# Attention in steps of four units instead of two, with eight probability buffers and one bank of sums

## What is computed

```python
def banded_attention(q, k, v, window, tab, sinks):
    ...
    logits = jnp.einsum('bgrnqd,bgnkd->bgrnqk', qb, kb).astype(jnp.float32) * (HEAD_DIM ** -0.5) + bias
    logits = jnp.where(valid, logits, NEG_INF)
    if sinks is None:
        probs = jax.nn.softmax(logits, axis=-1)
    ...
    out = jnp.einsum('bgrnqk,bgnkd->bgrnqd', probs.astype(v.dtype), vb)
```

## Time and profile before

| | |
|---|---|
| median of 3 runs | 4164.07 us (4163.08 to 4174.41) |
| the profiled execution | 4164.84 us, span 4162.8 us |
| PE, DVE, ACT busy over the span | 81%, 41%, 23% |
| granted PE clock, mean | 0.89 of 2.4 GHz |
| the five attention stages together | 414.5 us (A 99.1, B 41.5, C 52.4, S 110.2 and 111.3) |

### The profile page before, as it was taken

How to read it: one execution, slowest core, us unless ns; L and a number is a source line. 1 busy time by engine, 2 the same in 40 slices (tenths; PEclk the granted TensorE clock), 3 DMA queues, 4 the chain that set the end, 5 groups by cost and what they waited for, 6 DMA issues and landing times. The chain is left out here.

```text
span 4162.8 us, 48331 instructions
## 1 busy us (share of the span) xinstructions
PE 3381.5 (81%) x14856; PEld 2129.1 (51%) x14857; DVE 1702.3 (41%) x3938; ACT 966.0 (23%) x2034; POOL 326.0 (8%) x252
## 2 busy tenths in 40 slices
PE   4776859998997458996899999635789779999985
PEld 3644536666786326663444444413466534444443
DVE  2483553225342584225222222345832342222224
ACT  2263433223231223212111111012421301111111
POOL 0000000000000050000111111002300001111110
PEclk7788879999999678998899999867889989999997
DMA  3201011221312523310999999741422139999974
GB/s 119 80 1 67 26 48 46 89 81 54 114 65 67 179 101 92 81 36 35 372 403 406 400 394 400 287 156 41 152 57 86 51 127 412 399 404 392 386 292 181
DMA packets 286480, 747.29 MB, mean 180 GB/s; under 512 B 25475, under 2 KB 167181, under 8 KB 230132
## 3 DMA queue, kind: packets, MB, share of 16 engines
q1 hardware_dynamic: 258676, 677.81, 43.0%
q0 software_dynamic: 27648, 67.51, 4.1%
HBM read 719.71 MB, written 58.72 MB: 187 GB/s over the span
## 5 line engine op out<-in xcount | busy, mean ns | idle before, releaser
L2261 PE MATMUL up_ps<-experts,x_turned 128*64 128x512 f32 (+1 forms) x2256 | 696.7, 622 | 27.6 <-DMA experts<-in_w_up_dram 27.4
L2261 PEld LDWEIGHTS up_ps<-experts,x_turned 128*64 128x64 f32 (+1 forms) x2256 | 262.2, 160 | 385.0 <-issue 384.6
L242 DVE TENSOR_TENSOR pieces_lo<-weights,pieces_hi 128x512 fp32r<-128x512 f32 (+1 forms) x412 | 273.1, 683 | 329.3 <-ACT pieces_hi L236 327.6
L236 ACT CAST pieces_hi<-weights 128x512 fp32r<-128x512 f32 (+1 forms) x412 | 244.4, 614 | 463.4 <-PE products L254 102.2
L2285 PE MATMUL y_ps<-experts,hid_turned 128*64 128x512 f32 (+1 forms) x1128 | 345.6, 601 | 1.6 <-ACT hid_turned L2342 1.6
L2420 DVE TENSOR_TENSOR hid_seats<-up_ps,gated 128x256 f32<-128x256 f32 x94 | 57.6, 613 | 609.8 <-ACT gated L2335 609.8
L252 PE MATMUL gate_ps<-h_hi,pieces_hi 128*128 128x512 f32 x624 | 260.7, 418 | 35.5 <-DVE pieces_lo L242 29.1
L254 PE MATMUL gate_ps<-h_hi,pieces_lo 128*128 128x512 f32 x624 | 245.3, 393 | 0.0
L253 PE MATMUL gate_ps<-h_lo,pieces_hi 128*128 128x512 f32 x624 | 245.1, 393 | 0.0
L252 PE MATMUL products<-h_hi,pieces_hi 128*128 128x512 f32 x464 | 186.3, 402 | 69.1 <-DVE pieces_lo L242 69.1
L2285 PEld LDWEIGHTS y_ps<-experts,hid_turned 128*64 128x64 f32 (+1 forms) x1128 | 117.4, 154 | 222.3 <-issue 222.3
(11 more groups left out here) (413 smaller groups left out, 5294.8 us busy)
## 6 DMA issues: line engine op xcount, KB each, us to landing
experts<-in_w_gate_dram SPq DMA_DIRECT2D x141, 1024.0 KB, 10.2
experts<-in_w_up_dram SPq DMA_DIRECT2D x141, 1024.0 KB, 16.2
experts<-in_w_down_dram SPq DMA_DIRECT2D x141, 1024.0 KB, 15.4
weights<-in_w_ada_dram SPq DMA_DIRECT2D x24, 2048.0 KB, 7.9
rows_sb<-results SPq DMA_DIRECT2D x16, 2048.0 KB, 10.4
weights<-in_w_in_dram SPq DMA_DIRECT2D x57, 512.0 KB, 4.7
weights<-in_w_in_dram SPq DMA_DIRECT2D x12, 2048.0 KB, 7.9
weights<-in_w_out_dram SPq DMA_DIRECT2D x6, 2048.0 KB, 8.0
```

Of the source, the lines that this page charges most:

```text
L236: act.copy(self.like(view, self.hi[:, i % self.BUFFERS, :, :]), view).then_inc(s["hi_ready"], 1)
L242: dve.tensor_tensor(lo, view, hi.bitcast(F32), ALU.subtract).then_inc(s["lo_ready"], 1)
L2261: made = pe.matmul(up_ps[part, b, :].rearrange("p (h n) -> p h n", h=2), xT[:, b, k, part], experts.up(b + i)[:, :, k, :], start=(k == 0), ...
```

## The change

PE, DVE and the buffers change; the arithmetic of a unit does not.

- PE's loop goes over double steps q: scores of pairs 2q and 2q+1, turning of the four units 4q-4 to 4q-1, sums of pairs 2q-4 and 2q-3.
- DVE's loop goes over units: logits of u, scale of u-3, and `empty` of pair u/2-4 at even u; `add_row` once per unit.
- `prob` has eight buffers instead of six, `probT` eight instead of four, `turned` three banks instead of two, `summed` one instead of two. The waits that guard them follow these numbers. The first sums of a row m now wait for the copy of row m-1.
- ACT's order stays: the exponential of u, the copy of u-4.
- `vT` of each mixer lies in `oT`, and `right` has four slots for eight heads.

```diff
     nc = prog.nc
     with ExitStack() as ctx:
         scores = prog.ps(ctx, "scores", [P, 4, T])
-        turned = prog.ps(ctx, "turned", [P, 2, T])
-        summed = prog.ps(ctx, "summed", [P, 2, T])
-        prob = prog.sb(ctx, "prob", [P, 6, T])
-        probT = prog.sb(ctx, "probT", [P, 4, T])
+        turned = prog.ps(ctx, "turned", [P, 3, T])
+        summed = prog.ps(ctx, "summed", [P, T])
+        prob = prog.sb(ctx, "prob", [P, 8, T])
+        probT = prog.sb(ctx, "probT", [P, 8, T])
...
 
                 def turn(u):
                     pe.wait_ge(s["scaled"], u + 1)
-                    if u >= 2:
-                        pe.wait_ge(s["probsT_ready"], u - 1)
+                    if u >= 3:
+                        pe.wait_ge(s["probsT_ready"], u - 2)
                     c = 0
                     for i, (r, v) in enumerate(units[u]["v"]):
-                        last = pe.transpose(turned[0:r, u % 2, i * P:(i + 1) * P], prob[:, u % 6, c:c + r],
+                        last = pe.transpose(turned[0:r, u % 3, i * P:(i + 1) * P], prob[:, u % 8, c:c + r],
                                             prog.ident[:, :])
                         c += r
                     last.then_inc(s["turned_ready"], 1)
@@ -557,26 +557,28 @@
                     x = units[2 * p]
                     m, cols = x["tile"]
                     pe.wait_ge(s["probsT_ready"], 2 * p + 2)
-                    if m >= 2 and x["opens"]:
-                        pe.wait_ge(s["out_ready"], m - 1)
+                    if m >= 1 and x["opens"]:
+                        pe.wait_ge(s["out_ready"], m)
                     n = len(x["v"])
                     for i in range(n):
                         for side in range(2):
                             u = 2 * p + side
                             r, v = units[u]["v"][i]
-                            last = pe.matmul(summed[half(side), m % 2, cols], v, probT[0:r, u % 4, i * P:(i + 1) * P],
+                            last = pe.matmul(summed[half(side), cols], v, probT[0:r, u % 8, i * P:(i + 1) * P],
                                              start=(x["first"] and i == 0), stop=(x["last"] and i == n - 1))
                             if i == n - 1:
                                 last.then_inc(s["summed_ready"], 1)
 
-                for p in range(pairs + 3):
-                    if p < pairs:
-                        make_scores(p)
-                    if 2 <= p < pairs + 2:
-                        turn(2 * p - 4)
-                        turn(2 * p - 3)
-                    if p >= 3:
-                        weigh(p - 3)
+                for q in range(pairs // 2 + 2):
+                    if q < pairs // 2:
+                        make_scores(2 * q)
+                        make_scores(2 * q + 1)
+                    if 1 <= q <= pairs // 2:
+                        for u in range(4 * q - 4, 4 * q):
+                            turn(u)
+                    if q >= 2:
+                        weigh(2 * q - 4)
+                        weigh(2 * q - 3)
 
             @block.scalar
             def _(act):
...
-                    if u >= 4:
-                        act.wait_ge(s["summed_ready"], 2 * (u // 2) - 2)
+                    if u >= 8:
+                        act.wait_ge(s["summed_ready"], 2 * (u // 2) - 6)
                     vs = units[u]["v"]
                     r = vs[0][0]
-                    act.copy(probT[0:r, u % 4, 0:P * len(vs)],
-                             turned[0:r, u % 2, 0:P * len(vs)]).then_inc(s["probsT_ready"], 1)
+                    act.copy(probT[0:r, u % 8, 0:P * len(vs)],
+                             turned[0:r, u % 3, 0:P * len(vs)]).then_inc(s["probsT_ready"], 1)
 
                 for u in range(len(units) + 4):
                     if u < len(units):
...
@@ -639,7 +641,7 @@
                 def empty(p):
                     m = units[2 * p]["tile"][0]
                     dve.wait_ge(s["summed_ready"], 2 * p + 2)
-                    dve.tensor_copy(oT[:, m, :], summed[:, m % 2, :]).then_inc(s["out_ready"], 1)
+                    dve.tensor_copy(oT[:, m, :], summed[:, :]).then_inc(s["out_ready"], 1)
 
                 def add_row(n):
...
                 rows_left = 4 * (ADA - ADA_FIRST) if beside else 0
-                for p in range(pairs + 4):
-                    if p < pairs:
-                        logits(2 * p)
-                        logits(2 * p + 1)
-                    if 1 <= p <= pairs:
-                        scale(2 * p - 2)
-                        scale(2 * p - 1)
-                    if p - 4 in closes:
-                        empty(p - 4)
-                    for n in range(2 * p, min(2 * p + 2, rows_left)):
-                        add_row(n)
+                for u in range(len(units) + 9):
+                    if u < len(units):
+                        logits(u)
+                    if 3 <= u < len(units) + 3:
+                        scale(u - 3)
+                    if u % 2 == 0 and u // 2 - 4 in closes:
+                        empty(u // 2 - 4)
+                    if u < rows_left:
+                        add_row(u)
 
 
 def unit(q, k, n, v, tile, opens, closes, bias=None, extra=None, sink=None, minus_sink=None, factor=None, first=True,
...
-        right = prog.sb(ctx, "right", [P, H, T])
+        right = prog.sb(ctx, "right", [P, H // 2, T])
         c = at["c_v"]
         tiles = feature_tiles(ring, at["c_q"], 512, 0, qT)
```

More of the change, by code:

```diff
@@ L632, in scale @@
                     link(dve.reciprocal(a, m))
[L633 removed]
+                    probs = prob[:, u % 8, 0:x["n"]]
                     if x["factor"] is None:
@@ L1148, in mixer_c @@
                                       t == 0, t == TT - 1, bias=prog.causal[:, T - n:T],
-                                      extra=(left[side, tile[1]], right[side, h, 0:n])))
+                                      extra=(left[side, tile[1]], right[side, m, 0:n])))
         attention(prog, units, oT[:, 2, :, :])
```

21 lines of the change are left out of this document (10 added, 11 removed).

## The result

| | before | changed |
|---|---|---|
| median | 4163.59 us (4163.08 to 4174.41, 4 runs) | 4238.22 us (4236.35 to 4242.82, 4 runs) |
| the profiled execution | 4164.84, span 4162.8 | 4236.35, span 4234.3 |
| granted PE clock, mean | 0.89 | 0.88 |
| the five attention stages together | 413.0 | 491.5 |

The ratio is 1.0175, 95% interval 1.0156 to 1.0193: 74.6 us more, where the forecast was 40 and the range ended at 4236. The stages account for all of it (+78.5; the rest of the span took 7.0 less).

What follows compares the result with a forecast made beforehand. DVE was taken to bound B and late S, PE and its exchange with DVE to bound C, with A between. 12 + 8 + 2 + 18 = 40 us on 4164.84 gave 4204 us, range 4172 to 4236.

Steps and rivals of the forecast that it cites:

- B: DVE-bound attention stage: waits of 1.03 us for scores and 1.63 for sums at closing rows, +8 us.
- C: Attention stage bound by PE and its exchange with DVE: 12.3 us per row against 11.77, +2 over four rows.
- rival 4: Same waits with a fallen PE clock: tails in A and B paid twice, say 30 us more, 4234 us; chance 0.10.
- A: Attention stage: 1.31 us of waiting in 22 of 24 steps, 28.8; 111 us against 99.1, +12.
- the tails: Per double step, PE's turning, four units' sums and next scores; DVE waits this less one unit's work.
- S: Attention stage in two layers: full-clock sum 11 us per layer, bounds 0 and 16, taken as 9; +18 for both.
- that cover: In S, POOL proceeds while DVE waits for PE, so up to all waits of the first steps cost nothing.
- Removes: half of the changes of kind.: On PE, 112 pairs become 56 double steps, each sparing 0.55 us, together 31; worth nothing in B and S.
- rival 1: PE's gaps are the bound: 13 us come back in A, 4 in C, nothing in B and S, 4148; chance 0.08.

Runs made afterwards that it cites:

- the lag of two: Changed kernel with DVE's scaling two units behind its logits instead of three, order by unit kept: 4174.79 us, ratio 1.0012.
- the sums in front: Changed kernel with the sums of the four older units in front of the four turnings in PE's double step: 4171.00 us, ratio 1.0002.
- the run with PE kept busy: Changed kernel with four idle identity transpositions before the second, third and fourth turning of each group: 4232.74 us, ratio 1.0161.
- the last kernel: The mix with PE's pause before the experts filled by 80 identity transpositions, and 25 in each modulation stage: 4147.69 us, ratio 0.9944.
- the mix: Changed kernel with PE's sums first in A and S, last in B and C; DVE by unit in S, by pairs elsewhere: 4162.07 us, ratio 0.9988.

## Why the prediction was wrong in size and right in kind

- **Direction and mechanism: right.** DVE waits for scores behind each double step and for sums at each closing row; its busy time did not grow. Rows closing in B and C wait 1.59 and 2.25 at full clock, forecast 1.63 and 2.28. The runs with DVE in pairs, with the lag of two and with the sums in front each remove or shorten the waits in another way; each brings back 63 to 71 us of the median, and 80, 60 and 84 us in the stages.
- **The step that failed: the choice between forecast and rival 4.** "It drops to its lower level for good" was given 0.10, on the ground that PE would be busy 85 of 111 us in A. It did not drop for good but for part of the time, and most in B, to 0.58. I had priced the tails at full clock and put the clock's fall into a rival, although PE's new pauses came with the forecast itself: a share of the fall belonged in the sum. What it measured, by the run with PE kept busy: at least 4.7 us in A, 6.6 in B, 5.4 and 5.5 in the two S, 22 of the 38.5 us by which the stages exceed the forecast 40. Rival 4 gave 4234, and that this is near the measured 4238.2 is partly luck: its 30 us stood for A and B alone, where the clock's share was 11.3 by that run, and it had nothing for S. Nor were PE's pauses of 1 to 2 us: inside A of the changed kernel the longest is 0.84 us, and inside B but one (1.88) lasts at most 0.80.
- **B**: +8 forecast, +13.3 measured. The waits for scores were 2.4 us each for 1.03, the copies inside waited 1.59, 2.72 and 2.72 for 1.63. The run with PE kept busy has 0.97 and 1.59 throughout, and 48.2 in all against the forecast 49.5. The missing term is the clock, 6.6 us.
- **A**: +12 forecast, +25.6 measured. The clock is worth 4.7 by the same run. The rest is what the sum left out. In that run the waits for scores behind the tails are 28.1 us for 28.8 forecast, so this term was right (it has some of the filler's own time in it). The three copies inside A wait 1.63, 1.68 and 1.68, together 5.0, like B's, and I had priced them at nothing; the first scores and the last sums take 6.1 for 3.7; and 3.3 of idle around small instructions, which was there before, was left out.
- **C**: +2 forecast, +1.4 measured. Row 12.56 for 12.3.
- **S**: +9 each forecast, +19.0 and +19.3 measured, above the upper bound of 16. In the first layer DVE's idle time before copies rose from 2.7 to 18.6 and before logits from 4.4 to 12.8, 24.3 in all, and 5.5 us of its busy time came back, since less of it stood beside POOL: 18.8 together. I had taken that cover to be worth up to all of the first waits. The Trainium skill ("SBUF — State Buffer", SBUF: two separate sides) has the exclusion of the two engines on which I had built this. The trace agrees in direction, by these 5.5 us and no more. The copies wait 4.1 to 5.4, not 2.7, at a clock of 0.69; with PE kept busy and the clock at 1.00 one of them waits 2.68.
- **"Removes: half of the changes of kind."** I took them as worth something only if PE set the pace, and the run with DVE in pairs shows C 7.8 us faster than before, about twice the 4 that rival 1 gave it, and B 3.0 faster where it gave nothing; what share the deeper buffers have in this isn't shown. The Trainium skill's rule on changes of tiling mode ("TensorEngine Tiling (Array Packing)", Key Properties), that a change of mode drains the engine, points the right way, and the trace has pauses of 0.17 to 0.21 us at such changes; alone it doesn't tell the time, which hung on DVE's order.
- **Not priced**: the single bank of sums. In pair steps the kernel that has it is 28 us slower (ratio 1.0067, with the deeper buffers in it); in double steps nothing of it is visible.
- **The range**: its lower end does not follow from its reasons. Both S at 0 and half of A's 12 give 4164 + 6 + 8 + 2 = 4180, not 4172.

What stays open: why the clock returns early behind the 15.8 us pause in one layer and late in another, with the same instructions on both sides; and how the 13.6 us by which S exceeds its 110 even with PE kept busy divide between the clock, still at 0.74 and 0.76, and POOL.

## What to carry to other kernels

Where two engines hand work to and fro in fixed orders, count on each the units that lie between its last delivery of a group and its next demand on the other; that work must cover the other's whole queue in between (here one unit against a turning, four sums and scores). Change the step sizes of both engines together, or try each alone: here PE in double steps with DVE by unit took 4238 us, PE in pairs with DVE by unit 4272, and PE in double steps with DVE in pairs 4167. And when a forecast contains new pauses of PE, put a price for its clock into the sum, not beside it.

## What the runs showed of the hardware

- The granted clock of a stage fell with PE's short pauses, and came back when they were filled. In B it is 0.80 before (8 pauses of over 0.3 us without matmul or weight load, none over 0.6), 0.58 with a tail per double step (16) and 0.50 with one per pair (15, ten of them over 0.6); with idle matmuls in the pauses it is 0.91, at the same DVE order (3). Neither their length nor their number alone tells the clock: with DVE in pairs B has 7 pauses of 0.8 to 1.01 us and a clock of 0.87, and with PE in pairs C has 15 of over 0.3 and a clock of 0.94. At the lower level the pause between kinds of work is 0.33 us in place of 0.17.
- Dummy transpositions in a pause pay where PE has nothing else in it: in front of the experts 13.5 us of them in each of the two layers (with a few more in the other modulations) took 14 us off the kernel's time. In C, where PE sets the pace, they cost 3.3.
- Identical code behind an identical pause of 15.8 us took 7.3 or 12.7 us, sometimes both in the two layers of one execution. The span outside the five attention stages, where the edits changed next to nothing but in the last kernel, was 3742.7 to 3764.8 us over the profiled executions; a gain read from one stage's window can vanish in it, as the mix's did.
